# Sample outputs of a gated recurrence computed between the tiles of the last two gate products, and old states scaled by VectorE at the addition

## The reference

```python
def step(S, inp):
    qc, lfc, kc, vc = inp
    b = jnp.cumsum(lfc, axis=2)
    o_inter = jnp.einsum('bhtd,bhde->bhte', qc * jnp.exp(b), S)
    ...
    A = jnp.einsum('bhtd,bhsd,bhtsd->bhts', qc, kc, decay)
    o = o_inter + jnp.einsum('bhts,bhse->bhte', A, vc)
    bl = b[:, :, -1:, :]
    S = jnp.exp(bl[:, :, 0, :])[..., None] * S + jnp.einsum('bhsd,bhse->bhde', kc * jnp.exp(bl - b), vc)
    return S, o
...
o = rmsnorm(o, out_g.reshape(HG_HEADS, HG_DV))
o = o * jax.nn.silu(hg.astype(jnp.float32).reshape(B, T, HG_HEADS, HG_DV))
```

## Time and profile before

| | |
|---|---|
| median of 3 runs | 1194.55 us (1193.45 to 1194.9) |
| the profiled execution | 1190.76 us, of which 1189.0 us is the span of the records |
| TensorE busy | 1144.3 us, 96% of the span |
| VectorE, ScalarE, GpSimd busy | 570.3, 442.8, 351.3 us |
| mean granted clock of TensorE | 0.987 |

### The profile page before, as it was taken

How to read it: one execution, slowest core, us unless ns; L and a number is a source line. 1 busy time by engine, 2 the same in 40 slices (tenths; PEclk the granted TensorE clock), 3 DMA queues, 4 the chain that set the end, 5 groups by cost and what they waited for, 6 DMA issues and landing times.

```text
span 1189.0 us, 20688 instructions
## 1 busy us (share of the span) xinstructions
PE 1144.3 (96%) x8995; PEld 1025.0 (86%) x8995; DVE 570.3 (48%) x781; ACT 442.8 (37%) x739; POOL 351.3 (30%) x222
## 2 busy tenths in 40 slices
PE   5999999999999999999999999999999999999997
PEld 3997564456799999779999877999999999999997
DVE  5522354767436664476622443854445444512332
ACT  6423456667452125221531333233443344311111
POOL 0232110210333163144024101434444443334441
PEclk9999999989999999999999999999999999999999
DMA  5443330420624251214582534322323232313321
GB/s 183 129 145 99 98 107 1 142 72 1 247 72 149 71 176 45 71 54 136 193 327 72 193 151 154 105 74 77 102 73 106 72 107 72 106 63 98 96 65 76
DMA packets 91393, 130.13 MB, mean 109 GB/s; under 512 B 6676, under 2 KB 78728, under 8 KB 89000
## 3 DMA queue, kind: packets, MB, share of 16 engines
q1 hardware_dynamic: 83448, 101.71, 26.2%
q0 software_dynamic: 7856, 27.11, 6.8%
HBM read 120.38 MB, written 12.59 MB: 112 GB/s over the span
## 4 chain that ended last, share of the span: by engine, by line
PE 88%; DVE 5%; ACT 3%; DMA 2%; issue 1%; SPq 0%; DVEq 0%; ACTq 0%
PE ring L736 47%; PE hold L838 6%; PE ring L710 5%; PE ring L1232 2%; PE ring L1431 2%; PE ring L1147 2%; PE ring L1246 2%; PE ring L933 2%; PE ring L944 2%; PE hold L964 1%; PE ring L783 1%; PE ring L1380 1%; PE ring L1494 1%; PE ring L720 1%; PE ring L1513 1%
## 5 line engine op out<-in xcount | busy, mean ns | idle before, releaser
L629 POOL TENSOR_TENSOR weight_lo<-w_ring,weight_hi 128x1024 fp32r<-128x1024 f32 (+1 forms) x108 | 264.1, 2446 | 555.1 <-ACT weight_hi L1699 555.1
L1699 ACT ACTIVATE weight_hi<-w_ring 128x1024 fp32r<-128x1024 f32 (+1 forms) x135 | 140.5, 1041 | 438.0 <-PE ring L736 358.6
L736 PE MATMUL ring<-operand_hi,weight_hi 128*128 128x272 f32 (+1 forms) x1056 | 219.2, 289 | 0.3 <-ACT arena L1998 0.3
L736 PE MATMUL ring<-operand_lo,weight_hi 128*128 128x272 f32 (+1 forms) x1056 | 218.7, 288 | 0.0
L736 PE MATMUL ring<-operand_hi,weight_lo 128*128 128x272 f32 (+1 forms) x1056 | 217.6, 287 | 0.0
L736 PEld LDWEIGHTS ring<-operand_hi,weight_hi 128*128 128x128 f32 (+1 forms) x1056 | 164.6, 187 | 3.9 <-issue 2.8
L736 PEld LDWEIGHTS ring<-operand_hi,weight_lo 128*128 128x128 f32 (+1 forms) x1056 | 164.7, 187 | 0.4
L736 PEld LDWEIGHTS ring<-operand_lo,weight_hi 128*128 128x128 f32 (+1 forms) x1056 | 164.5, 186 | 0.4
L838 PE MATMUL hold<-arena,w_ring 128*128 128x504 f32 (+1 forms) x192 | 76.4, 516 | 1.2 <-DVE arena L2340 1.2
L1679 ACT ACTIVATE arena<-ring 128x1024 f32<-128x1024 f32 (+9 forms) x77 | 56.2, 738 | 55.0 <-PE ring L736 16.9
L2793 DVE TENSOR_TENSOR x_res<-x_res,ring 128x544 f32<-128x544 f32 x24 | 17.3, 720 | 119.8 <-PE ring L736 119.5
(11 more groups left out here) (440 smaller groups left out, 2196.6 us busy)
## 6 DMA issues: line engine op xcount, KB each, us to landing
w_ring<-in_w_in SPq DMA_DIRECT2D x13, 1024.0 KB, 5.4
w_ring<-in_ffn_w_gate SPq DMA_DIRECT2D x11, 1024.0 KB, 5.3
w_ring<-in_ffn_w_up SPq DMA_DIRECT2D x11, 1024.0 KB, 5.3
w_ring<-in_ffn_w_down SPq DMA_DIRECT2D x8, 1024.0 KB, 5.2
arena<-in_cache_mem_k SPq DMA_DIRECT2D x6, 1024.0 KB, 8.6
arena<-in_cache_mem_v SPq DMA_DIRECT2D x5, 1024.0 KB, 12.1
w_ring<-in_ca_wk SPq DMA_DIRECT2D x4, 1024.0 KB, 5.2
w_ring<-in_ca_wv SPq DMA_DIRECT2D x4, 1024.0 KB, 5.3
```

The lines of the kernel that those rows point to most:

```text
L629: self.ops.tensor_tensor(half_of(WL, self.x, kk, cols), w, half_of(WH, self.x, kk, cols).bitcast(F32), ALU.subtract).then_inc(sem("weights ...
L736: last = mm(ps[0:cols, hf * 512:hf * 512 + HALF], half_of((WH, WL)[pw], x, KT, cols)[:, i, :], (xh, xl)[px][:, k, hf * HALF:(hf + 1) * HAL ...
L1699: fn(half_of(WH, y, kk, cols), w, COPY).then_inc(sem("weights_hi"), 1)
```

## The change

- The sample part of the four outputs (8 matmuls of 4 columns and one with 32 rows per head) is made between the row blocks of the gate tiles 2 and 3, heads 0 and 1 in the one and 2 and 3 in the other, into a part of HOLD. `hg_output` keeps the prompt part.
- ScalarE copies the samples' outputs of all heads out of HOLD and squares them once; the squares of a head cover 512 columns. The squares of the memory tokens stand behind those of head 3 instead of head 2.
- VectorE gets `out_taken` for 512 columns mixed with `mixed_lo`, and `out_gate(3)` and `gates_ready` behind the third of them. Two small operations treat the samples of all heads.
- `state_scaled` leaves GpSimd. `state_new` does scaling and addition in one operation per sequence, 8 per head, each waiting for the one before.

```diff
+            def sample_outputs():
+                open_hold(("so",))
+                for h in range(HH):
+                    pe.wait_ge(sload[h], 16)
+                    o = sample_bank()[:, h]
+                    for b in range(DB):
+                        mm(o[:, DS * b:DS * b + DS], S0[:, h, b * HK:(b + 1) * HK],
+                           hQ[:, h, SEQ + DS * b:SEQ + DS * b + DS], start=(b == 0), stop=False, skip_group_check=True)
+                        if b % 2 and b < DB - 1:
+                            yield
...
             for m in range(HH):
-                split_product(("hg", m // 2, m % 2), open_item(("hg", m)), range(KT), OPH, OPL, nothing,
-                              True, True).then_inc(psum_full, 1)
+                split_product(("hg", m // 2, m % 2), open_item(("hg", m)), range(KT), OPH, OPL,
+                              between if m > 1 else nothing, True, True).then_inc(psum_full, 1)
...
+                if h == 0:
+                    act.wait_ge(hold_free, hold[("so",)] + 1)
+                    step(fn(hK[:, :, SEQ:TOK], osam, ACT.Square))
+                fn(hK[:, h, 0:SEQ], slot(key)[:, 0:SEQ], ACT.Square).then_inc(sem("o_squares"), 1)
+            act.wait_ge(hold_full, hold[("so",)] + 1)
+            fn(osam, sample_bank(), COPY).then_inc(hold_free, 1)
             for h in range(HH):
                 out_squares(h)
-                if h == 2:
+                if h == HH - 1:
                     act.wait_ge(sem("mem_in"), 16)
...
-                tt_(S0[:, h, :], S0[:, h, :], HOLD[:, :], ALU.add).then_inc(hold_free, 1)
+                for b in range(DB):
+                    at = slice(b * HK, (b + 1) * HK)
+                    ins = stt(S0[:, h, at], S0[:, h, at], T[2][:, h, SEQ // DS + b:SEQ // DS + b + 1], HOLD[:, at],
+                              ALU.mult, ALU.add)
+                    if b < DB - 1:
+                        step(ins)
+                    else:
+                        ins.then_inc(hold_free, 1)
...
-            for h in range(HH):
-                state_scaled(h)
```

More of the change, by code:

```diff
@@ L317, in plan @@
         hold += [("Ss", rd), ("PV", rd)]
-    hold += [("As",), ("osum",)] + [("rows", h) for h in range(HH)]
+    hold += [("As",), ("so",), ("osum",)] + [("rows", h) for h in range(HH)]
     hold += [("dSs", h) for h in range(HH)] + [("cS",), ("cO",)]
@@ L647, in freed, with sample_bank @@
             return psum_free[ring[key] % 3]
+        def sample_bank():
+            return HOLD[:, HALF:HALF + HH * NSMP].rearrange("p (h t) -> p h t", h=HH)
         def side_bank(key):
@@ L1298, in state_sums, with between @@
                 last.then_inc(psum_full, 1)
+            def sample_outputs():
[9 more added lines that the diff above has]
+                    if h == 0:
+                        pe.wait_ge(sem("values_in"), 2)
+                    last = mm(o, hi[0:NSMP, QT, h * HK:(h + 1) * HK], AS_[0:NSMP, h, :], start=False, stop=True,
+                              skip_group_check=True)
+                    if h < HH - 1:
+                        yield
+                last.then_inc(hold_full, 1)
+                yield
+            samples = sample_outputs()
+            def between(k):
+                next(samples, None)
             for m in range(HH):
-                split_product(("hg", m // 2, m % 2), open_item(("hg", m)), range(KT), OPH, OPL, nothing,
-                              True, True).then_inc(psum_full, 1)
+                split_product(("hg", m // 2, m % 2), open_item(("hg", m)), range(KT), OPH, OPL,
+                              between if m > 1 else nothing, True, True).then_inc(psum_full, 1)
                 if m == 0:
@@ L1321, in hg_output @@
                         mm(ps[:, cs], Sst[:, h, c - 1, :], hQ[:, h, cs], start=True, stop=False)
-                    mm(ps[:, cs], hi[:, c, hs], AP_[:, h, cs], start=(c == 0), stop=True)
-                for b in range(DB):
-                    mm(ps[:, 512 + DS * b:512 + DS * b + DS], S0[:, h, b * HK:(b + 1) * HK],
-                       hQ[:, h, SEQ + DS * b:SEQ + DS * b + DS], start=(b == 0), stop=False, skip_group_check=True)
-                mm(ps[:, 512:TOK], hi[0:NSMP, QT, hs], AS_[0:NSMP, h, :], start=False, stop=True,
-                   skip_group_check=True).then_inc(psum_full, 1)
+                    last = mm(ps[:, cs], hi[:, c, hs], AP_[:, h, cs], start=(c == 0), stop=True)
+                last.then_inc(psum_full, 1)
             def hg_sum(h):
@@ L2721, in _ @@
             state_scan(1)
-            for f in range(4):
-                mixed_lo(f)
-            out_gate(3)
-            dve.sem_inc(sem("gates_ready"), 1)
             def out_taken(h):
@@ L2730, in out_taken, with samples_taken @@
                 dve.wait_ge(sem("o_squares"), h + 1)
-                stt(MX[:, 4 + h, :], slot(key)[:, 0:TOK], GV[:, V_HG + h:V_HG + h + 1], hG[:, h, :], ALU.mult,
+                stt(MX[:, 4 + h, 0:SEQ], slot(key)[:, 0:SEQ], GV[:, V_HG + h:V_HG + h + 1], hG[:, h, 0:SEQ], ALU.mult,
                     ALU.mult).then_inc(freed(key), 1)
+            def samples_taken():
+                dve.wait_ge(hold_free, hold[("so",)] + 1)
+                o = MX[:, 4:4 + HH, SEQ:TOK]
+                step(tt_(o, osam, hG[:, :, SEQ:TOK], ALU.mult))
+                step(tt_(o, o, bc(GV[:, V_HG:V_HG + HH], 2, NSMP), ALU.mult))
             def out_scaled(h):
@@ L2741, in state_new @@
                 dve.wait_ge(hold_full, hold[("dSs", h)] + 1)
-                dve.wait_ge(sem("state_scaled"), h + 1)
-                tt_(S0[:, h, :], S0[:, h, :], HOLD[:, :], ALU.add).then_inc(hold_free, 1)
+                for b in range(DB):
[6 more added lines that the diff above has]
+                        ins.then_inc(hold_free, 1)
                 dve.wait_ge(hold_free, hold[("dSs", h)] + 1)
                 dve.sem_inc(sem("state_new"), 1)
-            for h in range(3):
-                out_taken(h)
+            out_taken(0)
+            mixed_lo(0)
+            mixed_lo(1)
+            out_taken(1)
+            mixed_lo(2)
+            mixed_lo(3)
+            out_taken(2)
+            out_gate(3)
+            dve.sem_inc(sem("gates_ready"), 1)
+            samples_taken()
+            out_taken(3)
             dve.wait_ge(sem("mem_squares"), 2)
@@ L2754, in _ @@
                 ts(mst[:, m, :], mst[:, m, :], mrs[:, m:m + 1], None, ALU.mult).then_inc(sem("mem_scaled"), 1)
-            out_taken(3)
             dve.wait_ge(hold_full, hold[("osum",)] + 1)
@@ L3047, in values_diag @@
                                 ALU.mult).then_inc(sem("v_diag"), 1)
-            def state_scaled(h):
-                full(pool, ("o", h))
-                x = S0[:, h, :].rearrange("p (b e) -> p b e", b=DB)
-                g.tensor_tensor(x, x, bc(T[2][:, h, SEQ // DS:TOK // DS], 2, HK), ALU.mult).then_inc(
-                    sem("state_scaled"), 1)
             def state_out(h):
```

5 lines of the change are left out of this document (2 added, 3 removed).

## The result

The changed kernel takes 1209.86 us (median of 6 runs, 1207.56 to 1215.88); the kernel before, run beside it, takes 1195.04 (1193.45 to 1197.03). The ratio is 1.0139, 95% interval 1.0113 to 1.0166: slower by 1.4%, or 16.6 us. The forecast was 1207.7 in a range of 1201.0 to 1213.5, with 0.94 for slower. The profiled execution took 1208.68 us with a span of 1206.9, which is 17.9 more than the 1189.0 of before.

The account below looks back on a forecast made before the run. TensorE, busy 1144.3 of 1189.0 us, was taken to bound the kernel. Later rows 8.4 (9.3 - 0.9), clock 3.0 and new states 1.8 made 13.2 us: 1204.0 profiled, 1207.7 as a median, range 1201 to 1213.5.

Parts of the forecast that it names:

- Term 1: Sample matmuls moved into gate tiles 2 and 3 are paid in full, with operand switches: gate tile 3 ends 9.3 us later.
- G: The end of gate tile 3, at 467.22 us before the change and forecast at 476.5 after it.
- Term 2: Side chain from G to `rows_of_norm`: 28.0 us instead of 28.9; TensorE arrives at G + 21.0 and idles some 7 us.
- Term 3: Low clock behind the wait before `rows_of_norm(0)`: rows 0, transposes and rows 1 cost 3.0 us more; what follows ran low before.
- Term 4: New states on VectorE: 8 operations take 3.0 us where one took 1.23, +1.8 us on the path for head 0.
- C: Rival: the clock stays at 2.4 GHz through the wait before the rows; 1199.8 us, chance 0.08.
- D: Rival: the memory load is not late, `hg_rstd` is ready when TensorE arrives at G + 21; 1191.6 us, chance 0.03.
- E: Rival, part of D: the load is down a few us sooner and the clock does not suffer; 1195.5 us, chance 0.03.

Follow-up runs that it names:

- gate first: The changed kernel with VectorE making the last gate and releasing the memory load ahead of its first `out_taken`: 1200.49 us, ratio 1.0081 to the kernel before.
- filled wait: The changed kernel with fourteen extra fp32 matmuls of 256 columns ahead of `rows_of_norm(0)`, in TensorE's long wait: 1207.48 us, ratio 1.0123 to the kernel before.
- the states alone: The kernel before with only the new states changed: no scaling on GpSimd, 8 VectorE operations per head; 1198.50 us, ratio 1.0055.
- memory later: The reordered kernel with the memory tokens' mean and scaling behind the second head's rows: 1190.39 us, ratio 0.9983 to the kernel before.
- reordered: The changed kernel with last gate, memory release and heads' norm moved ahead, states scaled early, ScalarE's first squares before the last sigmoid: 1193.08 us, ratio 1.0028 to before.
- tiles only: The changed kernel with VectorE's order, memory squares and GpSimd state scaling of before, only the sample outputs moved: 1198.71 us, ratio 1.0074 to before.
- one group: The changed kernel with each gate tile's samples in one group ahead of its first row block: 1208.57 us, ratio 1.0152 to the kernel before.
- after without samples: The changed kernel without the 32 four-column sample matmuls: ratio 1.0072 to the kernel before.
- early scaling: The changed kernel with VectorE scaling the old states ahead of time in four wide operations: 1205.25 us, ratio 1.0111 to the kernel before.
- norm first: The changed kernel with the heads' mean and norm ahead of the memory tokens', `mem_t(0)` behind `rows_of_norm(3)`: 1205.51 us, ratio 1.0106 to the kernel before.

## Why the prediction was right, and where its terms were off

The direction, the place and the main wait were right: the tiles stretched (from 6.1 to 10.5 us each), a wait of 2.10 us at `hg_sum(0)`, the load late, and 6.33 us of idle time before the rows. That the median fell well inside the range is luck in part. The sum was 13.2 us where 16.4 to 16.6 were measured, with one term of 5.0 us missing and 2.1 us too many in another:

- **Term 1, 9.3 us.** From the transposes ahead of gate tile 2 to G it takes 26.3 us (451.25 to 477.55) against 17.5 (449.72 to 467.22): 8.8. The matmuls paid most of their price, 0.34 for a group where 0.42 was charged, and the switch 0.10 instead of 0.08; the pair of products behind a 32-row matmul takes another 0.1. The pair of kernels without them (8.0 us and nothing told) shows that they are paid in the tiles and that taking them away behind G gains nothing. The profile of after is another 1.5 us later where the stretch begins; that is inside the 6.6 us by which its start differs among the fourteen profiles.
- **Term 2, rows at G + 28.0.** They start at G + 29.05. The square came at G + 6.9 (6.8), but the release of the memory slot at G + 13.5 instead of 12.4. Between them the clock fell to 1.2 GHz for 3.4 us behind the wait for that square, `hg_output(2)` came late, and VectorE stood 1.27 us for its third square (the row at 489.66). From there on every step is as worked out: load 5.06 us, squares, scaling in 1.42 at the smaller of the two bounds, since GpSimd no longer works beside it. The wait on the chain is in good part the order's doing: with the gate first the rows come 3.9 us sooner after G. TensorE came to them at G + 22.7 and not at G + 21.0, for the low clock that I had taken out of its work (1.7 us) came again elsewhere.
- **Term 3, 3.0 us.** The three steps cost what was said: 2.15 + 1.90 + 2.12 against 1.11 + 1.02 + 1.11, +2.9. The step that failed is that what follows would be low as before. It came back sooner: rows 3 take 1.33 instead of 2.11 and the 24 matmuls 3.21 instead of 4.46, -2.0. Net +0.9. Its cause was half right: in this kernel the clock did fall in the wait, but the filled wait shows that it falls without one too, some 3 us later against the rows and for as long.
- **Term 4, 1.8 us.** 3.03 against 1.23 us, to the digit. But I priced the wait and not what it does. Term 3 said that a wait brings the clock down and term 4 lengthened a wait on TensorE from 0.56 to 2.38 us; the two were never put together. The second fall costs 0.8 in the transposes, 1.8 in the state product and half of the 4.85 us of low clock in the product behind: 5.0 us. Together 6.8; the third length says 6.5, and the states alone give 6.6 by the ratio (4.0 to 9.1) and 5.0 by their third length.

Terms measured: 8.8 + 0.15 + 0.9 + 1.8 + 5.0 = 16.65, against 16.4 by the three lengths and 16.6 by the ratio. Rivals C, D and E did not come. C could have looked true from the wait's end: the clock read 1.00 in it (500.0 to 505.5), and was low at the first matmul behind.

What stays open: why the low stretch behind the rows was 3.4 us long in one kernel (memory later), 6.8 in the reordered, 10.2 before and with the tiles only, 13.6 or 13.7 in seven, and 20.5 in three, with nearly the same instructions in it. Short waits between the rows (0.92 and 0.81) went with the shortest, but a wait of 0.81 is in all fourteen profiles, and no run varied the other alone.

## What to carry to other kernels

Work that stands behind the last large product, while other engines make the next operand, can be free; moved into the product it was paid nearly in full, and the side chain then started later by the same amount. To make such a move good the side chain has to be shortened, and for that the order on each of its engines has to be changed, not on one: reordered on VectorE alone it brought the rows 4 us sooner, on VectorE, ScalarE and TensorE 9. Even so the best version here can't be told from the kernel before. And when a small operation grows in front of a waiting TensorE, price the clock behind the wait as well: here 1.8 us of VectorE cost 5.0 to 6.6.

## What the hardware did that I had not expected

- The clock fell while TensorE's records show no gap: behind 4.40 of 4.40 busy us of sample matmuls (one group). It fell also 2.2 us into rows and transposes that followed 6.2 us of fp32 matmuls, with one gap of 0.65 us (filled wait).
- A wait of 2.4 us went with 1.2 GHz, at its end or within 0.9 us, in seven profiles of seven, one of 0.57 us in none of seven, at one and the same place. At the rows, waits of 5.8 to 7.7 us and one of 2.47 found the clock low at the first matmul, waits of 0 to 0.86 us found it high. The wait of 2.21 us between two rows of the reordered kernel found it high as well (a row of 1.18 us), and the clock fell 1.1 us after the wait.
- VectorE's four `mixed_lo` took 4.49, 6.72 and 8.42 us with one, two and three of GpSimd's scalings beside them, 2.63 where none was: 1.9, 4.1 and 5.8 us more, where one scaling alone takes 1.90. An edit that gives TensorE less to do (the kernel before without the samples) lengthened them in this way.
- The same 1 MB load of the memory tokens took 5.06, 5.44, 6.42 and 8.23 us in four kernels that issue it behind the same operation of VectorE (the changed kernel, after without samples, early scaling, norm first). No run shows why.
